# Turning the cached keys on VectorE in 32x32 blocks, keeping them in HBM, and scoring an iteration at once

## The reference

```
past_k = cache_sb_k[l][page_table].reshape(DB, past_len, SB_HEADS, SB_DIM)
k_all = concatenate([past_k, k_new], axis=1)
z = einsum('bqhd,bkhd->bhqk', q, k_all) * scale + bias
log_1mb = where(mask, log_sigmoid(-z), 0)
tail = cumsum(log_1mb, reverse=True) - log_1mb
w = where(mask, exp(log_sigmoid(z) + tail), 0)
o = einsum('bhqk,bkhd->bqhd', w, v_all)
```

## Time and profile before

| | |
|---|---|
| median of 3 runs | 1406.8 us (1406.1 to 1408.73) |
| profiled execution: span, first to last instruction | 1407.3 us; for this one nothing is recorded around the span |
| PE busy | 1391.1 us (99%) |
| PEld, DVE, ACT, POOL busy | 1321.4, 899.6, 734.5, 182.6 us |
| DMA | 249.41 MB, mean 177 GB/s; HBM written 5.53 MB |
| granted TensorE clock, mean | 0.998 |

### The profile page before, as it was taken

The page is one execution under the profiler, slowest core; times in us unless marked ns, Lnnn a source line. Parts: engine busy times, 40 slices in busy tenths (PEclk is TensorE's granted clock), DMA queues, the critical chain, the costliest instruction groups (busy, mean ns, idle before and its releaser), DMA issues.

```text
span 1407.3 us, 26950 instructions
## 1 busy us (share of the span) xinstructions
PE 1391.1 (99%) x10551; PEld 1321.4 (94%) x10551; DVE 899.6 (64%) x1508; ACT 734.5 (52%) x1210; POOL 182.6 (13%) x333
## 2 busy tenths in 40 slices
PE   7999999999999999999999999999999999999998
PEld 6999999988878999999999999999888799999998
DVE  5666544669995876663367665346899858756542
ACT  4544434489766554443365444346887665444441
POOL 1020000323262110000000000021433510000000
PEclk9999999999999999999999999999999999999999
DMA  9575455577799595545545555564868895555541
GB/s 247 150 210 150 141 147 153 156 203 230 210 310 265 145 255 150 150 139 152 155 127 149 151 149 144 152 175 141 252 206 242 287 255 154 151 149 149 148 139 50
DMA packets 391554, 249.41 MB, mean 177 GB/s; under 512 B 16513, under 2 KB 379638, under 8 KB 391428
## 3 DMA queue, kind: packets, MB, share of 16 engines
q1 hardware_dynamic: 375602, 204.94, 51.2%
q0 software_dynamic: 15520, 42.62, 9.7%
q10 hardware_dynamic: 306, 0.13, 0.0%
HBM read 242.10 MB, written 5.53 MB: 176 GB/s over the span
## 4 chain that ended last, share of the span: by engine, by line
PE 94%; DVE 2%; ACT 1%; DMA 1%; issue 1%; SPq 0%; POOLq 0%; POOL 0%; DVEq 0%; ACTq 0%
PE bank L596 25%; PE bank L598 24%; PE bank L597 24%; PE bank L862 3%; PE bank L973 2%; PE bank L877 2%; PE bank L632 2%; PE bank L636 2%; PE bank L633 2%; PE bank L1050 1%; DMA raw<-in_ffn_w_gate 1%; PE bank L827 1%; PE bank L954 1%; PE bank L1168 1%; PE bank L1090 1%
## 5 line engine op out<-in xcount | busy, mean ns | idle before, releaser
L1602 DVE TENSOR_TENSOR w_l<-raw,w_h 128x1024 fp32r<-128x1024 f32 (+1 forms) x332 | 395.4, 1196 | 295.4 <-ACT w_h L1224 295.1
L596 PE MATMUL bank<-hh,w_h 128*128 128x320 f32 x1632 | 512.9, 314 | 0.0
L598 PE MATMUL bank<-hh,w_l 128*128 128x320 f32 x1632 | 504.4, 309 | 0.0
L597 PE MATMUL bank<-hl,w_h 128*128 128x320 f32 x1632 | 504.3, 309 | 0.0
L1224 ACT ACTIVATE w_h<-raw 128x1024 fp32r<-128x1024 f32 (+1 forms) x332 | 332.3, 1030 | 141.4 <-DMA raw<-in_ffn_w_down 101.4
L596 PEld LDWEIGHTS bank<-hh,w_h 128*128 128x128 f32 x1632 | 306.4, 188 | 11.8 <-issue 8.6
L597 PEld LDWEIGHTS bank<-hl,w_h 128*128 128x128 f32 x1632 | 306.5, 188 | 0.6
L598 PEld LDWEIGHTS bank<-hh,w_l 128*128 128x128 f32 x1632 | 306.4, 188 | 0.0
L596 PE MATMUL bank<-guh,w_h 128*128 128x320 f32 x704 | 217.7, 309 | 0.0
L598 PE MATMUL bank<-guh,w_l 128*128 128x320 f32 x704 | 217.4, 309 | 0.0
L597 PE MATMUL bank<-gul,w_h 128*128 128x320 f32 x704 | 217.4, 309 | 0.0
(11 more groups left out here) (297 smaller groups left out, 1604.9 us busy)
## 6 DMA issues: line engine op xcount, KB each, us to landing
raw<-in_ffn_w_gate SPq DMA_DIRECT2D x88, 512.0 KB, 4.0
raw<-in_ffn_w_up SPq DMA_DIRECT2D x88, 512.0 KB, 3.9
raw<-in_ffn_w_down SPq DMA_DIRECT2D x64, 448.0 KB, 3.8
raw<-in_w_in SPq DMA_DIRECT2D x44, 512.0 KB, 4.0
raw<-in_ffn_w_down SPq DMA_DIRECT2D x32, 512.0 KB, 4.0
kpg<-in_cache_sb_k SPq DMA_DIRECT2D x112, 128.0 KB, 3.3
kpg<-in_cache_sb_k POOLq DMA_DIRECT2D x112, 128.0 KB, 2.7
raw<-in_w_out SPq DMA_DIRECT2D x16, 512.0 KB, 6.9
```

Source lines behind the costliest of these rows:

```text
L596: pe.matmul(out, w_h[:, slot, k, :], rhs_h[:, k0 + k, :], start=first, stop=False)
L597: pe.matmul(out, w_h[:, slot, k, :], rhs_l[:, k0 + k, :], start=False, stop=False)
L598: last = pe.matmul(out, w_l[:, slot, k, :], rhs_h[:, k0 + k, :], start=False, stop=end)
L1602: V(dve.tensor_tensor(w_l[:, slot, 0:n, :], raw[:, slot, 0:n, :], w_h[:, slot, 0:n, :].bitcast(F32), ALU.subtract), sm["w_lo"])
```

## The change

- Keys are loaded as rows during an FFN by POOL: a unit of work is four pages of one sequence, loaded by four DMAs of 128 KB. Each goes to 32 partitions only, with four rows of 1 KB on each. A single DVE instruction (`dve.transpose`, 1024 elements on each of 128 partitions) turns its 32x32 blocks, and four DMAs of 128 KB, in pieces of 512 B, store the result to a new HBM tensor `turned_keys`. Two buffers.
- There are 32 such units per layer. For layer 0 all are done in the first FFN: one behind each of 20 gate/up steps (from the second pair on), and two in each of the first six down steps. For layer 1: 16 in the FFN at the end of layer 0 and 16 in the first FFN of layer 1.
- In the mixer SP and POOL load an iteration as four DMAs of 512 KB, 4 KB on a partition, straight into `kT`. `turn_keys`, `copy_keys`, `turn_keys_early`, `kpz`, `kpg` and the early copies are gone. `scores(it)` is 8 matmuls of 512 columns, into banks 4 and 2 by turns, at the m at which the second half's scores were placed before.
- The constants' DMAs share one semaphore, POOL starts after 8 units of weights and not after 16, and it waits for all stores before it goes on to the mixer's own loads and memsets.

```diff
+SCORES_AT = {9: 0, 10: 1, 12: 2, 13: 3, 15: 4, 17: 5, 19: 6, 21: 7}
+SCORE_BANK = (4, 2)
...
+    turned_keys = nc.dram_tensor("turned_keys", [L, ITS, G, P, 2, 4, P], F32, kind="Internal").ap()
...
# SP, mixer (POOL: the same for b in (2, 3), with kt_used alone as its wait)
+                def keys(it):
+
                     for b in (0, 1):
-                        if h < 4:
+                        if it < 2:
                             sp_.wait_ge(sm["w_used"], U + U_IN + 4)
                         else:
-                            sp_.wait_ge(*at("kt_turned", 4 * (h - 2) + b + 1))
-                        for j in range(2):
-                            sp_.dma_start(heads(kpg[l][:, h % 2, b, j, :]), page(sp_, ids[4 * b + 2 * (h % 2) + j], ins["cache_sb_k"], l)).then_inc(sm[f"ks_loaded{h % 2}"], 16)
+                            sp_.wait_ge(*at("kt_used", it - 1))
+                        sp_.wait_ge(sm[f"kx_stored{b}"], 64 * (l * UNITS_K // 2 + 2 * it + 1))
+                        sp_.dma_start(kT[l][it % 2][:, b], turned_keys[l, it, b].rearrange("p a n s -> p a (n s)")).then_inc(sm[f"ks_loaded{it % 2}"], 16)
...
# POOL, FFN
+                def load_rows(i):
+
+                    g = l * UNITS_K + i
+                    if g >= 2:
+                        pool.wait_ge(sm["kx_turned"], g - 1)
+                    page_ids(pool, ids, i // G, (i % G,))
+                    for n in range(4):
+                        pool.dma_start(kn_[32 * n:32 * n + 32, g % 2], quarter(pool, ids[n], ins["cache_sb_k"], l)).then_inc(sm[f"kn_loaded{g % 2}"], 16)
+
+                def store_turned(i):
+
+                    g = l * UNITS_K + i
+                    pool.wait_ge(sm["kx_turned"], g + 1)
+                    for n in range(4):
+                        pool.dma_start(turned_keys[l, i // G, i % G, :, :, n, :].rearrange("(r p) a s -> p a r s", p=32),
+                                       kx_[32 * n:32 * n + 32, g % 2].rearrange("p (a r) s -> p a r s", a=2)).then_inc(sm[f"kx_stored{g % 2}"], 16)
...
+                load_rows(0)
+                load_rows(1)
+                for i in range(UNITS_K):
+                    store_turned(i)
+                    if i + 2 < UNITS_K:
+                        load_rows(i + 2)
+                all_stored(pool, l)
...
# PE, mixer
-                def scores(h):
+                def scores(it):
+
+                    pe.wait_ge(*at(f"ks_loaded{it % 2}", 32 * (it // 2 + 1)))
+                    pe.wait_ge(*at(f"kp_loaded{it % 2}", 32 * (it // 2 + 1)))
...
+                            last = pe.matmul(out[32 * b:32 * b + 32, :], qb[:, p_, c0:c0 + 32], kT[l][it % 2][:, b, p_, :],
                                              start=(p_ == 0), stop=(p_ == 1), skip_group_check=True)
...
# DVE, FFN
+            def turn_keys(k2, units):
+
+                for _ in range(units):
+                    if staged[0] >= (1, 1.5, 2, 2)[k2] * UNITS_K:
+                        return
+                    g = staged[0]
+                    dve.wait_ge(sm[f"kn_loaded{g % 2}"], 64 * (g // 2 + 1))
+                    if g >= 2:
+                        dve.wait_ge(sm[f"kx_stored{g % 2}"], 64 * (g // 2))
+                    V(dve.transpose(kx_[:, g % 2].rearrange("p c (j s) -> p j c s", s=32), kn_[:, g % 2].rearrange("p j (c d) -> p j c d", d=32)), sm["kx_turned"])
+                    staged[0] += 1
...
                         V(dve.tensor_tensor(gul[:, 2 * i + t, :], gt[:, t, :], guh[:, 2 * i + t, :].bitcast(F32), ALU.subtract), sm["gu_lo"])
+                        if i and (k2 == 0 or t == 0):
+                            turn_keys(k2, 1)
...
+                    if n < KD - 2:
+                        turn_keys(k2, 2 if k2 == 0 else 1)
```

More of the change, by code:

```diff
@@ L303, in build @@
     assert a[0] >= end_ffn and gul_at + 11 * T * 4 <= st_at and st_end <= gul_end
[L304 removed]
+    k_at = [end_ffn]
+    kn_ = sb("kn_", [P, 2, 4, 256], at=k_at)
+    kx_ = sb("kx_", [P, 2, 8, P], at=k_at)
+    assert k_at[0] <= nc.sbuf_usable_end
     wT = sb("wT", [P, ITS, 4, P], at=[a[0]])
@@ L446, in _ @@
                     load_in(m + 3)
-                    for h in range(4, 2 * ITS):
-                        if SLOT_OF[h - 2] == m:
-                            keys(h)
+                    for it in range(2, ITS):
+                        if SCORED[it - 2] == m:
+                            keys(it)
                 for it in range(ITS):
@@ L745, in ffn @@
                 post_mean(M)
[L747 to L759, removed]
-                            last = pe.transpose(bank[b_][:, p_ * 256 + j * P:p_ * 256 + (j + 1) * P], kpz[:, h, b, j, p_ * P:(p_ + 1) * P], cst_("ident"))
-                    last.then_inc(sm["kt_turned"], 1)
-            def keys_early_copied(l2, h):
-                pe.wait_ge(sm["kt_copied"], 64 * l2 + 4 * h + 4)
             for l in range(L):
@@ L1013, in _ @@
                         gate_rows(u, out, range(4))
-                    elif h == last_h:
+                    else:
                         unit(u, out, hh, hl, part=range(4))
-                    else:
-                        unit(u, out, hh, hl, part=range(3))
-                        turn_keys(h, (2, 3))
-                        unit(u, out, hh, hl, part=range(3, 5))
-                        turn_keys(last_h, (0, 1))
-                        unit(u, out, hh, hl, part=range(5, 6))
-                        scores(h)
-                        unit(u, out, hh, hl, part=range(6, 7))
-                    if last_h < 2 * ITS:
-                        turn_keys(last_h, (2, 3))
                     if m == 9:
@@ L1044, in _ @@
                     else:
-                        unit(u, out, hh, hl, part=range(4, KD) if h == last_h else range(7, KD))
+                        unit(u, out, hh, hl, part=range(4, KD))
                 def gla_outputs(pair):
@@ L1926, in _ @@
                         place_prompt(m - 13)
-                    for h in TURNS[m]:
-                        if h >= 2 and h % 2 == 0:
-                            log_weights(h // 2 - 1)
+                    if m in SCORES_AT:
+                        log_weights(SCORES_AT[m])
                     if m == NIN - 1:
```

201 lines of the change are left out of this document (70 added, 131 removed).

## The result

| | before | after |
|---|---|---|
| median of the runs, us | 1407.39 (4 runs, 1406.1 to 1408.73) | 1425.98 (4 runs, 1424.76 to 1428.06) |
| ratio after/before, 95% interval | | 1.0133 [1.0118, 1.0147] |
| span of the profiled execution, us | 1407.3 | 1424.5 (time of this execution 1426.12) |

The change makes the kernel 1.3% slower, where 1% faster was forecast.

What follows compares the result with a forecast made beforehand. PE was taken to bound the kernel, with DVE taking over in the mixers. 1407.3 less 20.5 us for the mixers plus 6 for the first FFN's DMA gave 1393 us; range 1376 to 1432.

Steps and rivals of the forecast that it cites:

- DMA: this is the dear part ... I take 6.: First FFN: gate/up steps just fit the DMA rate, down steps do not; a loss of 6 us.
- c: First FFN: assumed DMA rate in MB/us; 0.292 costs 6 us, 0.30 is just covered, 0.34 makes nothing late.
- My formula: First FFN: lateness of 20 gate/up and 6 down steps, 63.3/c - 199, with about 12 us covered by the eight slots.
- my own sign of being wrong: First FFN: PE waits of more than 20 us would show the forecast wrong.
- Rival (a): First FFN becomes DMA-bound through 32-partition transfers, kernel slower: 1429 us at c = 0.25, 1455 at half rate; chance 0.20.
- POOL 5.0 us per unit: FFNs: POOL's issue of four loads and four stores takes about 5.0 us per unit of keys.
- DVE's turn 1.2 us: FFNs: each DVE transpose of 1024 elements takes 1.2 us, with 0.6 and 2.4 as ends.
- Cost nothing: FFNs: DVE's added transposes stay hidden, 5.4 us busy per 7.0 us gate/up step, 6.3 per 9.7 us down step.
- Mixers 20.5 us: Both mixers: a gain of 10.5 us in layer 0 and 10 in layer 1, with DVE taking over as bound.
- Loads in the mixer "may lose 1 us per layer": Mixer front: DVE's `lo` of m = 8 may lose 1 us per layer, lying within the 20.5.
- Scores: Mixer: 16 calls of twice the columns at 1.86 us, 29.8 us against 32.0, 2 us off PE.
- The other two FFNs free: Two other FFNs carry half the key load, 223 GB/s in gate/up and 257 in down steps: no cost.

Runs made afterwards that it cites:

- f5: Kernel after with key loads over 128 partitions, every key in its place, stores still one per 32 partitions: median 1402.1 us, ratio 0.9958 to the kernel before.
- e2: Kernel after with key loads and stores both spanning 128 partitions, same bytes and pieces, keys in another order: 1403.8 us.
- f2: Kernel after with only the key loads spanning 128 partitions, stores at 32, keys in another order: 1400.3 us.
- e4: Kernel after with only the first of four stores per turned unit issued; the mixer loads other cache rows in as many bytes: 1408.3 us.
- f1: Kernel after with loads and stores over 128 partitions and every key in its place, scores reading a strided view: 1448.1 us.
- g1: f5 with 8 of the 15 convolution taps left out in each mixer: span 1380.3 us against f5's 1396.4.
- f4: f1 with the weights of m = 8 and 9 queued ahead of the keys of iteration 1: 1453.4 us.
- e3: Kernel after with POOL issuing the loads of unit i + 2 ahead of the stores of unit i: 1430.4 us.
- f3: Kernel after with only the stores spanning 128 partitions, key loads at 32: 1417.6 us.
- f7: f5 with POOL's loads started after 4 weight units instead of 8 and 3 turns moved out of the down steps: 1406.3 us, ratio 0.9988.
- h2: f5 with only POOL's start earlier, after 4 weight units instead of 8: 1400.9 us, ratio 0.9959.
- h3: f5 with the weights of m = 8 and 9 queued between the keys of iterations 0 and 1: 1397.6 us.
- e1: Kernel after with only 16 of layer 0's 32 key units turned, the same bytes loaded in the mixer: 1396.6 us.

## Why the forecast was wrong, step by step

- **"DMA: this is the dear part ... I take 6."** This is the step that failed; it cost 28.1. The steps' needs (298 and 366 GB/s) and the bound were right, and so was the place: PE full to 165 us, late behind. Too high was the rate. I took c = 0.292, just under the lower of two rows (293 and 340 GB/s) whose transfers span 128 partitions, for transfers that touch 32. It was 0.281 in 130 to 165 and 0.284 in 165 to 262 us. My formula gives with these 20 x (2.1/0.281 - 7.0) + 6 x (3.54/0.284 - 9.7) - 12 = 14 us. The rest is in its form. From 165 to 282 us PE was busy 93.2 of 117.2 us, so it idled 24.0 where it had idled 0.8 before; and what it did took 93.2 where it had taken 88.3, which is the clock at its lower level, 1.2 GHz, three times in and right behind the stage, for 10.2, 6.8 and 10.2 us, each begun in a wait (rows in the last section). The formula has neither the wait that DVE passes on to the next split nor the clock, about 5 us; the 9 us that are left are not separated further. f5 shows the same gap in the form: at its 307 GB/s the formula gives nothing, and the stage lost 4.8 us. PE's 24 us of waits were also my own sign of being wrong, "more than 20 us".
- **Rival (a)** named the right property and gave 0.20 to it, with 1429 us at c = 0.25. That this lies 3 us from the measured time is luck: its 42 us for the stage were 14 too many, and the 20.5 us that it took off for the mixers 9.5 too many. By e2 and f2 the partitions of the loads make 22.4 of the 28.1 us. But the row that it was built on was one of stores, and with loads over 128 partitions the stores over 32 cost nothing (f2 against e2). The Trainium skill, SBUF - State Buffer, Door 1: The DMA port swizzle, halves such a transfer's bandwidth; read strictly this gave 1455, and the runs show a mean over both queues of 281 against 305 GB/s, where half of the bytes are weights. With the loads at 32 and few stores, in e4, it is 234.
- **POOL 5.0 us per unit**: 4 x 0.552 + 4 x 0.613 = 4.7. Right, and no guide to f1, where the stores' form made it 18.
- **DVE's turn 1.2 us**: 1.24. Right. "Cost nothing" holds for the work, not for its wait, with PE's splits behind it.
- **Mixers 20.5 us**: 11.0. That DVE would take over was right (39.0 of 40 and 19.5 of 20 us in the fences above, g1). The size was wrong twice. First, DVE had less to give: f5 gains 8.2 and 7.5 us where I had 10.5 and 10. In the first 40 us of layer 0's mixer DVE was busy 25.9 us before and 26.1 in f5, so its idle time there was not to be had; the gain is 33.0 to 39.0 in the next 40, and some 2 us in 120 to 160. Second, the kernel after lost 2.8 us more in layer 0. Up to the matmul that waits for `qt`, 131 us behind the entry, the two kernels are level to 0.2 us; the rest takes 80.5 us after and 77.4 in f5. In that rest the clock of the kernel after is 0.91 in both 422 to 442 and 442 to 462 us, f5's 1.00 in the like stretches; in layer 1 (1.9 us more than f5) it is 0.91 in one of them. The other traces go the same way in layer 0: 80.2 and 80.3 us in e4 and f4, where the clock fell twice there too, and 76.9 to 77.2 in e3, f1, f2, f3, f7 and h2, where it did not (78.8 and 78.5 in e2 and h3, with one fall each; e1, without one, has 78.5 too). A late first FFN is not what brings it about: e3 and f3 end theirs at 291.2 and 278.1 us and have mixers of 208.0 and 207.7. What does is open.
- **Loads in the mixer "may lose 1 us per layer"**: h3 shows no gain from an earlier w_in, and no wait of PE for `kT` shows in the kernel after. **Scores** 29.8 us: 256 matmuls with a mean of 0.598 us, four side by side, keep PE busy 7.7 us for each of the four tiles of keys, 30.8 in all. Right.
- **The other two FFNs free**: 474.2 against 474.2. Right.

## What to carry to other kernels

Before a stage is given a second stream of transfers, work out its bytes per step against a rate measured with transfers of the same shape, and expect a transfer into 32 partitions to slow the others beside it; choose the layout so that loads span all 128, and let the compute engine's addressing put things right (f5: same bytes, same turns, 24 us less). An in-order engine that waits for such a transfer must have nothing behind it that the bound engine needs soon. And what can be won by unloading one engine is the idle time of the next one in that very stretch, taken stretch by stretch, not its sum.

## What the runs showed of the hardware

- Key loads into 32 partitions beside the weights: 281 GB/s at a share of 1.13; the same loads over 128 partitions: 305 at 1.00. In the mixer, with 4 KB per partition, the kernel after reached 372 GB/s for 4 us (344 to 348).
- POOL's issue of a DMA went from 0.6 to 2.1 us for a store in f1's form, and the plain loads queued behind it to 2.4.
- TensorE's clock fell to its lower level, 1.2 GHz, while it stood still for 8.4 us, and came back some 5 us after it had work again, so that a wait costs more than its own length (the kernel after, first FFN):

```profile
181.00:185.00 4.00, 0.00 (x0) 0.00 (x0) 2.98 (x4) 0.96 (x3) 3.03 (x7) 0.83 1.13 289
185.00:189.00 4.00, 0.00 (x0) 0.00 (x0) 3.26 (x5) 2.74 (x4) 3.58 (x7) 0.50 1.14 264
189.00:193.00 4.00, 3.82 (x14) 3.82 (x15) 2.48 (x3) 2.38 (x3) 1.52 (x4) 0.50 1.11 317
193.00:197.00 4.00, 4.00 (x27) 4.00 (x26) 1.09 (x1) 0.58 (x2) 3.41 (x6) 0.89 1.14 257
```

- The clock also fell where PE was busy 20.00 of 20.00 us (0.91 in 422 to 442); no run shows why.
- f5 scatters more than the kernel before beside it: 1398 to 1408 us against 1406.8 to 1411.8. Apart from the one of 3756.6 us, its two longest executions, 1406 and 1408 us, have a mean clock of 0.985, the five of 1398 to 1403 us 0.987 to 0.990. Full DMA engines alone don't make it: the kernel after, fuller than f5 there, kept within 1424.8 to 1428.1 in four.
